# The moving operands of both blocks' matmuls, each pair of chunks begun at another column

## The reference, cut to what matters

```
# first block, x is 256 x 2048
h    = rmsnorm(x) * (1 + scale) + shift          # scale, shift, gate from c @ w_ada
proj = h @ w_in                                  # 2048 x 9296: q, k, v, z of two attentions, index q, k, w
ya, yb = two attentions of 8 heads, times silu(z)
x    = x + gate * (concat(ya, yb) @ w_out)       # 2048 x 2048
# second block, 16 meta rows put ahead: 272 x 2048
z    = rmsnorm(r) @ w_in_2 + b                   # 2048 x 8200
m    = sigmoid(g1) * (attn @ w_attn_o) + sigmoid(g2) * (pool @ w_pool_o)
r    = r + rmsnorm(m @ w_out_2)
a    = causal_conv3(rmsnorm(r) @ w_ffn_up)       # 2048 x 11264
r    = r + rmsnorm((gelu(gate) * val) @ w_ffn_down)   # 5632 x 2048
```

## Time and profile before

| what | value |
|---|---|
| runs | 2021.78 and 2027.02 us, median 2024.4 us |
| the profiled execution, its own time | 2024.87 us |
| its span, first to last instruction | 2023.1 us |
| TensorE matmuls, busy | 1986.8 us (98%), 15340 |
| VectorE busy | 1292.1 us (64%) |
| ScalarE busy | 986.2 us (49%) |
| mean granted TensorE clock | 0.994 |
| DMA | 391.75 MB, 194 GB/s |

### The profile page before, as it was taken

The page is one execution under the profiler, slowest core; times in us unless marked ns, Lnnn a source line. Parts: engine busy times, 40 slices in busy tenths (PEclk is TensorE's granted clock), DMA queues, the critical chain, the costliest instruction groups (busy, mean ns, idle before and its releaser), DMA issues.

```text
span 2023.1 us, 39414 instructions
## 1 busy us (share of the span) xinstructions
PE 1986.8 (98%) x15340; PEld 1892.6 (94%) x15340; DVE 1292.1 (64%) x1670; ACT 986.2 (49%) x1434; POOL 139.2 (7%) x148
## 2 busy tenths in 40 slices
PE   6999999999999999999999999999999999999998
PEld 5989999999999999999999999999999999988886
DVE  6686778775677543444447664676777677665555
ACT  4244455564645544444444555654544445444444
POOL 0000000000002000000004111000010000000000
PEclk9999999999999999999999999999999999999999
DMA  9997866565455555655554655366556656655553
GB/s 353 318 331 235 288 209 211 183 202 167 152 166 173 167 176 158 180 157 147 150 149 151 207 189 187 104 189 198 186 176 196 198 176 189 216 199 192 190 192 140
DMA packets 188103, 391.75 MB, mean 194 GB/s; under 512 B 11955, under 2 KB 17632, under 8 KB 185568
## 3 DMA queue, kind: packets, MB, share of 16 engines
q1 hardware_dynamic: 186992, 388.03, 59.8%
q10 hardware_dynamic: 1024, 2.51, 0.4%
HBM read 388.39 MB, written 2.10 MB: 193 GB/s over the span
## 4 chain that ended last, share of the span: by engine, by line
PE 90%; DVE 4%; DMA 3%; ACT 1%; SPq 1%; issue 1%; DVEq 0%; ACTq 0%
PE acc L839 20%; PE acc L841 20%; PE acc L840 20%; PE acc L1268 2%; PE acc L1270 2%; PE acc L1269 2%; PE psum_y L840 2%; PE psum_x L840 2%; PE psum_y L841 2%; PE psum_x L839 2%; PE psum_x L841 2%; PE psum_y L839 2%; DMA ada_w<-in_w_ada 2%; DVE w_lo L1866 1%; DMA raw<-in_w_in 1%; PE psum_y L1268 1%
## 5 line engine op out<-in xcount | busy, mean ns | idle before, releaser
L1866 DVE TENSOR_TENSOR w_lo<-raw,w_hi 128x1024 fp32r<-128x1024 f32 (+1 forms) x644 | 810.8, 1272 | 603.1 <-ACT w_hi L1332 600.0
L1332 ACT ACTIVATE w_hi<-raw 128x1024 fp32r<-128x1024 f32 (+1 forms) x644 | 671.3, 1049 | 788.4 <-PE acc L841 482.3
L839 PE MATMUL acc<-act_hi,w_lo 128*128 128x258 f32 (+2 forms) x3424 | 969.8, 283 | 10.1 <-DVE w_lo L1866 6.0
L841 PE MATMUL acc<-act_hi,w_hi 128*128 128x258 f32 (+2 forms) x3424 | 957.2, 280 | 0.0
L840 PE MATMUL acc<-act_lo,w_hi 128*128 128x258 f32 (+2 forms) x3424 | 956.6, 279 | 0.0
L839 PEld LDWEIGHTS acc<-act_hi,w_lo 128*128 128x128 f32 x3424 | 645.4, 188 | 20.9 <-issue 10.4
L840 PEld LDWEIGHTS acc<-act_lo,w_hi 128*128 128x128 f32 x3424 | 645.8, 189 | 0.6 <-issue 0.5
L841 PEld LDWEIGHTS acc<-act_hi,w_hi 128*128 128x128 f32 x3424 | 644.8, 188 | 0.0
L839 PE MATMUL psum_x<-act_hi,w_lo 128*128 128x258 f32 x352 | 97.8, 278 | 0.0
L839 PE MATMUL psum_y<-act_hi,w_lo 128*128 128x258 f32 x352 | 97.5, 277 | 0.0
L840 PE MATMUL psum_x<-act_lo,w_hi 128*128 128x258 f32 x352 | 97.5, 277 | 0.0
(11 more groups left out here) (328 smaller groups left out, 2274.4 us busy)
## 6 DMA issues: line engine op xcount, KB each, us to landing
raw<-in_w_in SPq DMA_DIRECT2D x272, 512.0 KB, 3.7
raw<-in_w_ffn_up SPq DMA_DIRECT2D x176, 512.0 KB, 4.5
raw<-in_w_ffn_down SPq DMA_DIRECT2D x88, 512.0 KB, 3.5
ada_w<-in_w_ada SPq DMA_DIRECT2D x64, 512.0 KB, 10.0
raw<-in_w_out SPq DMA_DIRECT2D x64, 512.0 KB, 4.1
ada_x<-in_w_ada SPq DMA_DIRECT2D x16, 1024.0 KB, 6.4
raw<-in_w_attn_o SPq DMA_DIRECT2D x16, 512.0 KB, 3.7
raw<-in_w_pool_o SPq DMA_DIRECT2D x16, 512.0 KB, 4.6
```

The costliest lines, as they stand in the source:

```text
L839: pe.matmul(out, w_lo, a_hi, start=c == 0, stop=False)
L841: ins = pe.matmul(out, w_hi, a_hi, start=False, stop=last)
L1332: act.activation(M.hi[s][:, 0:job.width], M.raw[s][:, 0:job.width], ACT.Copy).then_inc(M.hi_ready[s], 1)
L1866: dve.tensor_tensor(M.lo[s][:, 0:job.width], M.raw[s][:, 0:job.width], M.hi[s][:, 0:job.width].bitcast(FP32), ALU.subtract).then_inc(M.lo_ ...
```

## The change

The first block's chunk k begins 6 (k // 2) columns further on than before, 24 bytes more for each pair, and its two tiles are 48 columns longer. The second block's chunk k begins at 320 k plus a number from a table of eight, one for each pair, where it was 320 k + 9 for all; the fourth of the eight is 9. `act_lo` of the first block moves 256 bytes and the tiles behind it (those placed from `ada_at`) 512 bytes. Every writer and reader goes through the same functions. No instruction, wait or DMA is added or taken away.

```diff
-INTO = 9
+INTO2 = (3, 5, 7, 9, 11, 30, 33, 42)
...
+def place1(k):
+
+    return SEQ * k + 6 * (k // 2)
...
-    M.act_hi = put("act_hi", [P, DC * SEQ], F32R, act_at)
-    M.act_lo = put("act_lo", [P, DC * SEQ], F32R, act_at + DC * SEQ * 4)
+    M.act_hi = put("act_hi", [P, DC * SEQ + 48], F32R, act_at)
+    M.act_lo = put("act_lo", [P, DC * SEQ + 48], F32R, act_at + DC * SEQ * 4 + LINE)
...
-    ada_at = act_at + 2 * DC * SEQ * 4
+    ada_at = act_at + 2 * DC * SEQ * 4 + 2 * LINE
...
     def act(k):
-        return M.act_hi[:, SEQ * k:SEQ * k + SEQ], M.act_lo[:, SEQ * k:SEQ * k + SEQ]
+        return M.act_hi[:, place1(k):place1(k) + SEQ], M.act_lo[:, place1(k):place1(k) + SEQ]
...
     def act2(k, c0, n):
-        return M.act2_hi[:, INTO + PITCH * k + c0:INTO + PITCH * k + c0 + n], M.act2_lo[:, INTO + PITCH * k + c0:INTO + PITCH * k + c0 + n]
+        return M.act2_hi[:, INTO2[k // 2] + PITCH * k + c0:INTO2[k // 2] + PITCH * k + c0 + n], M.act2_lo[:, INTO2[k // 2] + PITCH * k + c0:INTO2[k // 2] + PITCH * k + c0 + n]
...
     def hi_of(k):
-        return M.act_hi[:, SEQ * k:SEQ * k + SEQ]
+        return M.act_hi[:, place1(k):place1(k) + SEQ]
 
     def hi2_of(k, n):
-        return M.act2_hi[:, INTO + PITCH * k + ROWS - n:INTO + PITCH * k + ROWS]
+        return M.act2_hi[:, INTO2[k // 2] + PITCH * k + ROWS - n:INTO2[k // 2] + PITCH * k + ROWS]
```

More of the change, by code:

```diff
@@ L1906, in dve_program @@
     sq = lambda c: M.sq[:, (c % 4) * SEQ:(c % 4 + 1) * SEQ]
[L1907 to L1910, removed]
+    part_hi = lambda k: M.act_hi[:, place1(k):place1(k) + SEQ].bitcast(FP32)
+    part_lo = lambda k: M.act_lo[:, place1(k):place1(k) + SEQ]
+    part2_hi = lambda k, n: M.act2_hi[:, INTO2[k // 2] + PITCH * k + ROWS - n:INTO2[k // 2] + PITCH * k + ROWS].bitcast(FP32)
+    part2_lo = lambda k, n: M.act2_lo[:, INTO2[k // 2] + PITCH * k + ROWS - n:INTO2[k // 2] + PITCH * k + ROWS]
     dve.wait_ge(M.consts, 1)
```

## The result

The changed kernel takes 2059.5 us (median of two runs, 2058.6 and 2060.4) against 2024.4: a ratio of 1.0165, 95% interval 1.0125 to 1.0204. It is slower by 35 us, where 2031 was forecast. That lies in the range stated (2000 to 2068), but outside the forecast's own range (2020 to 2045). At 2% the comparison is unclear, since the interval reaches past 1.02; that the kernel is slower than before is clear of noise. The profiled execution has a span of 2058.6 us. In the code after, L839 to L841 are L844 to L846.

What follows compares the result with a forecast made beforehand. The prediction took TensorE's distance between matmul starts as the bound. Terms of +2.3 (256 columns), -2.8 (272) and +7.4 (258) sum to +6.9 us, giving 2031 us; range 2000 to 2068, its own 2020 to 2045.

Steps and rivals of the forecast that it cites:

- the dearest rival: All moved matmuls pay their upper bounds, 2071 us, slower by 2.3%; chance 15%.
- the leading case: Forecast of mixed prices over the moved matmuls with a small net loss, 2031 us, own range 2020 to 2045; chance 45%.
- 258 columns: Second block, 6132 matmuls: 1.2 ns dearer each, +7.4 us, bounds -8.6 to +28.2; sign: up's mean 116 to 118 ns.
- 256 columns: First block, 3354 matmuls: from 114.9 to a mix near 115.6 ns, +2.3 us, bounds -5.4 to +15.1.
- What bounds the kernel: TensorE, busy 1986.8 of 2023.1 us: time is the number of matmuls by the distance between two starts.
- The list of what moves: Count by jobs: 3354 matmuls of 256, 1386 of 272 and 6132 of 258 columns move; attention, out_a, attn_o, down stay.
- The slow mode broken by the new place: First block's lower bound: all at 113.3 ns, no whole panel at 117.8, since places change every 24 matmuls; -5.4 us.
- 272 columns: Second block, 1386 matmuls: 2 ns less each, -2.8 us, bounds -9.3 to +2.9; sign: mean under 126.7 ns.
- places near the `o` rows: Moving reads conflict with the weight load at most starts; all moved matmuls pay upper bounds, 2071 us; chance 15%.
- place inert: The dear `o` comes from the 64-byte jump between high and low parts; pairs run as today, 2024 us; chance 20%.
- better places: Overheads of moved matmuls fall to the least row and the slow mode doesn't hold, 2001 us; chance 20%.
- The rule against it: Skill page: TensorE never waits at its SBUF ports, so place would be worth nothing; new 16-byte lines pay a penalty.

Runs made afterwards that it cites:

- uniform_7: The kernel before the change with all pairs of the second block at column 7 in place of 9: 2054.7 us, ratio 1.0139.
- weights32: Against the changed kernel, the high and low weight tiles lie 32 bytes (8 columns) further and both blocks get other places: 2060.2 us.

## Why the prediction was right, and where its size was off

The time fell into the range because the range took in the dearest rival, not because the sum was right: the sum gave +6.9 us, and the change cost 35. Of the three signs named for the leading case, 258 columns in up failed (119.9 ns, not 116 to 118), 256 columns failed (118.8, not near 115.6), and only 272 held (under 126.7).

**What bounds the kernel** held: same counts, same other engines, and the whole difference in the distance between TensorE's starts. The list of what moves held too; the jobs that don't move kept their pace.

**256 columns** were mis-sized: +2.3 us in the sum, +9.6 measured. I took an even mix of two paces seen on one place (115.6). The seven new places gave 116.6 to 121.8, a mean of 118.8 over their pairs, within the bound of 119.4; the same pairs had 114.4 before. That would be 3354 x 4.4 = 14.7 us. The stages show 9.6: some of the rest is the clock in z_b, and v_a_low and v_b_low, interrupted by other work and with the DMA share above 0.9, hardly grew (30.2 and 30.1 us before, 30.4 and 29.9 after). "The slow mode broken by the new place" did come true, since no panel stands at 117.8 from end to end, but the new places are as dear as the slow mode.

**272 columns**: -2.8 in the sum, -0.9 measured. Places 3, 7 and 11 gained 1.5 to 3.5 ns, 42 lost 1.1, and the rest stayed near 126.7.

**258 columns** is the term that failed: +7.4 in the sum, +27.0 measured, near the upper bound of 28.2. I argued that four places within 6 columns of the old one would stay near its pace. The map shows that nearness counts for nothing: 8 and 10 are at 118.7 and 120.0, 9 at 115.6. And I put `o` (120.2) far off, since its place changes with each chunk. Its pace turned out to be that of ordinary places, six of the seven new ones being at 120.

So the rival "places near the `o` rows", which had 15%, was what happened: most places cost about what `o` does, and the old ones were among the few cheap ones. The experiment with the weights moved shows that the pace depends on the places of moving operand and weights together. That the two reads get in each other's way is the reading that fits; no row shows such a wait itself. Its price of 2071 us was 11 too high, for 272 columns went the other way, pair 3 stayed good, and 256 columns lay under their bound. The rival "place inert" falls with uniform_7, "better places" with the map.

**The rule against it.** At 258 columns 8 bytes of shift turned 115.6 ns to 120.0 (9 to 7), and 32 bytes of shift of the weights turned place 17 from 120.1 to 115.6. The Trainium skill, SBUF — State Buffer, section "SBUF: two separate sides", gives TensorE two independent read ports that wait on nobody; by it these shifts would be worth nothing. The measurement decides against that conclusion, though no row shows whether the time is lost at the ports. That page's penalty for new 16-byte lines doesn't order the places either: at 256 columns place 16 begins on such a line and has 120.0, place 23 begins in the middle of one and has 116.4.

## What to carry to other kernels

In a stream of matmuls like this one (float32 operands split in two, a weight load before each), the place of the moving operand relative to the stationary one in 256 bytes is worth 2 to 9% of TensorE's time (117.8 to 123.4 against 115.6 ns, 116.4 to 123.4 against 113.3). Good places are narrow: wherever a neighbour of one was measured (8 and 10, 12 and 14, 0 and 2 at 258 columns, 45 at 256), it was no better than the rest. Give every chunk the one place that was measured best for its column count, with a pitch of whole 256 bytes. What that brings is limited by where one starts: here the old places were already near the best. One kernel with eight places in a table measures eight prices at once, read from windows cut at each pair; a place's price can shift by 1 to 3 ns with the pair ahead of it, as places 5 and 30 showed.

## What was not expected of the hardware

- The commonest distances lie on steps. The three matmuls of a tile take 340, 346.7, 353.3, 360, 366.7 ns (113.3, 115.6, 117.8, 120.0, 122.2 each): steps of 6.67 ns, 16 columns at 2.4 GHz. Over all twelve traces some 65% of the undisturbed pairs are within 0.5 ns of such a step; the others lie between (118.7 at 258 columns, 123.3 at 272).
- One place can hold more than one pace. Place 0 at 256 columns ran at 113.3 or 117.8 ns, down at 228.8 ns in ten traces and at 233 in two (uniform_7, none of whose down tiles moved, and weights32), and place 5 at 120.0 or 123.1 by its neighbour. Place 9 (258 columns) was back at 115.6 in every run that had it. What chooses the pace stays open, and so does why 1, 9 and 13 are good: the runs show which distances are, and no rule that would foretell them.
